# Seven block products for the queries, keys and values of the forgetting attention, in place of a product per 128 tokens

## The reference, cut to what matters

```python
h = rms_norm(x, norm_mix_g[l])                      # x: (1, 512, 1024)
(f_q, f_k, f_v, f_f, n_q, ...) = split_cols(h @ w_in[l])   # f_q, f_k, f_v: 512 columns each
qa = rms_norm(to_heads(f_q, FOX_HEADS), fox_q_g[l])  # 8 heads of 64
ka = rms_norm(to_heads(f_k, FOX_HEADS), fox_k_g[l])
va = to_heads(f_v, FOX_HEADS)
log_f = jax.nn.log_sigmoid(f_f.astype(jnp.float32) + b_forget[l])
out_a = from_heads(fox_attention(qa, ka, va, log_f)) @ w_fox_up[l]
```

## Time and profile before

| | |
|---|---|
| median of 3 runs | 1430.56 us (1430.36 to 1430.82) |
| the profiled execution | 1434.81 us, its span 1433.5 us |
| busy: PE, PEld, DVE, ACT, POOL | 95%, 55%, 40%, 24%, 25% of the span |
| PE products of whole tiles (L467), 320 passes | 142.7 us |
| PE block products (L1592), passes of 128x256, first group 288 | 65.0 us |
| POOL sums of blocks (L1400), groups of 56 and 28 | 72.9 and 36.8 us |

### The profile page before, as it was taken

How to read it: one execution, slowest core, us unless ns; L and a number is a source line. 1 busy time by engine, 2 the same in 40 slices (tenths; PEclk the granted TensorE clock), 3 DMA queues, 4 the chain that set the end, 5 groups by cost and what they waited for, 6 DMA issues and landing times. The chain is left out here.

```text
span 1433.5 us, 24217 instructions
## 1 busy us (share of the span) xinstructions
PE 1361.1 (95%) x10188; PEld 785.7 (55%) x10188; DVE 567.9 (40%) x1394; ACT 351.1 (24%) x832; POOL 359.9 (25%) x426
## 2 busy tenths in 40 slices
PE   7999999899999997999999979999999999999997
PEld 3545544567888645444444434456877545555543
DVE  3235423573141534521211133545459582333415
ACT  2225324553101011111111123354221301322221
POOL 3050402205372561122222120220232003111062
PEclk9999999999999997999999999999999999999999
DMA  6175013310222348899999991010140331300131
GB/s 213 56 275 203 1 61 88 139 42 5 102 75 86 136 162 296 314 375 356 382 379 380 387 336 63 15 67 2 59 176 30 85 122 39 127 3 17 56 122 59
DMA packets 99791, 210.95 MB, mean 147 GB/s; under 512 B 14613, under 2 KB 22640, under 8 KB 99552
## 3 DMA queue, kind: packets, MB, share of 16 engines
q1 hardware_dynamic: 87152, 171.39, 33.0%
q0 software_dynamic: 12528, 37.97, 7.9%
HBM read 188.88 MB, written 19.42 MB: 145 GB/s over the span
## 5 line engine op out<-in xcount | busy, mean ns | idle before, releaser
L467 PE MATMUL pb<-Wt,HT 128*128 128x512 f32 x320 | 142.7, 600 | 0.6 <-DMA Wt<-in_w_in_dram 0.6
L3708 PE MATMUL pb<-Wt,HT 128*128 128x512 f32 x256 | 117.8, 602 | 0.2 <-DVE AR L3799 0.2
L1400 POOL TENSOR_TENSOR AR<-Wt,AR 128x512 f32<-128x512 f32 x56 | 72.9, 1323 | 122.6 <-PE pb L1592 89.5
L467 PEld LDWEIGHTS pb<-Wt,HT 128*128 128x128 f32 x320 | 60.0, 192 | 70.6 <-issue 70.5
L766 ACT ACTIVATE AR<-AR,SM 128x512 f32<-128x512 f32 (+3 forms) x128 | 70.8, 554 | 62.3 <-DVE SM L724 61.5
L2266 PE MATMUL pb<-AR 128*64 128x512 f32 x256 | 85.0, 595 | 0.7 <-issue 0.7
L724 DVE CUSTOM_DVE_ANT_0 AR<-pb,AR 128x512 f32<-128x512 f32 (+3 forms) x128 | 58.3, 487 | 64.4 <-PE pb L678 63.9
L1400 POOL TENSOR_TENSOR AR<-Wt 128x512 f32<-128x512 f32 x28 | 36.8, 1333 | 166.8 <-DMA Wt<-in_w_in_dram 81.0
L3708 PEld LDWEIGHTS pb<-Wt,HT 128*128 128x128 f32 x256 | 46.4, 190 | 52.0 <-issue 49.2
L2266 PE MATMUL pb<-Wt,AR 128*64 128x512 f32 x192 | 70.8, 595 | 0.0
L678 PE MATMUL pb<-AR 64*128 64x512 f32 (+7 forms) x256 | 62.5, 493 | 7.9 <-DVE SM L724 5.0
(11 more groups left out here) (575 smaller groups left out, 2400.5 us busy)
## 6 DMA issues: line engine op xcount, KB each, us to landing
Wt<-in_w_in_dram SPq DMA_DIRECT2D x18, 2048.0 KB, 9.5
AR<-in_w_gate_dram SPq DMA_DIRECT2D x8, 2048.0 KB, 17.3
AR<-in_w_up_dram SPq DMA_DIRECT2D x8, 2048.0 KB, 16.0
AR<-in_w_down_dram SPq DMA_DIRECT2D x8, 2048.0 KB, 13.6
Wt<-in_w_gate_dram SPq DMA_DIRECT2D x6, 2048.0 KB, 15.3
Wt<-in_w_down_dram SPq DMA_DIRECT2D x6, 2048.0 KB, 12.4
Wt<-in_w_up_dram SPq DMA_DIRECT2D x6, 2048.0 KB, 22.4
ys<-AR POOLq DMA_DIRECT2D x2, 3072.0 KB, 24.8
```

The costliest lines, as they stand in the source:

```text
L467: r = mm(s[:, 0:n], lT[:, k, t * 128:(t + 1) * 128], w[:, k, c0:c0 + n], start=k == 0, stop=k == nk - 1)
L1400: r = gt.tensor_tensor(out[:, k:k + s, :], a[:, k:k + s, :], b[:, k:k + s, :], op)
L3708: r = mm(s, HT[:, k, t * 128:(t + 1) * 128], W.ap(("gate2", c, br))[:, k, :], start=k == 0, stop=k == 7)
```

## The change

Queries, keys and values become three units of `Quarters` (`fq7`, `fk7`, `fv7`, L1592 there L1720). The queries' weights are loaded first, in place of the values', and their first two products p1 and p2 stand between the turns of the first norm. The four quarters of the result (c11 of tokens 0 to 255 and columns 0 to 255, and so on) take the place of the four tiles in the head norm: the first is read from PSUM, the three others from SBUF, where DVE has put them. The norm's scratch moves. POOL gets 24 sums of blocks: the queries' and keys' before the running sums are stored, the values' after the clearing of rows and before the masks; one of the broadcasts and its masks move to the end. The weights' slots come free at other products.

```diff
-        for name in ("fox_v", "fox_q", "fox_k", "nsa_q", "nsa_kv"):
+        for name in ("fox_q", "fox_k", "fox_v", "nsa_q", "nsa_kv"):
             W.plan(name, 8, 512)
...
-            load("fox_v", wcols(a["w_in"][0], 1024, 512))
+            load("fox_q", wcols(a["w_in"][0], 0, 512))
...
         def norm1_pe():
-            pipe(ALLT, norm1.turn_pe, lambda t: fox_v_pe(t) if t < 2 else None)
+            norm1.turn_pe(0)
+            norm1.turn_pe(1)
+            for t in range(2):
+                norm1.turned(t, pe)
+            fq7.p1_pe()
+            norm1.turn_pe(2)
+            fq7.p2_pe()
+            norm1.turn_pe(3)
             columns_pe()
...
+        def block_norm_ve(u, tag, b, s):
+            turned = ("turn", tag, b - 2) if b > 1 else (("turn", "fq", b + 2) if tag == "fk" else None)
+            if b == 0:
+                ht8.norm_ve(P.ap(u.key("x")), P.free(u.key("x")), s, turned)
+            else:
+                ht8.norm_ve(flat((u.c12, u.c22, u.c21)[b - 1]), None, s, turned)
+
+        def fox_qkv_pe():
+            q, k, v = fq7, fk7, fv7
+            q.p5_pe()
+            gates_pe()
+            q.p6_pe()
+            block_turn_pe(q, "fq", 0)
+            q.p3_pe()
+            running_sums_pe()
+            q.p7_pe()
+            k.p1_pe()
+            q.p4_pe()
+            block_turn_pe(q, "fq", 1)
+            k.p5_pe()
+            block_turn_pe(q, "fq", 2)
+            k.p2_pe()
+            block_turn_pe(q, "fq", 3)
...
+            k.p6_pe()
+            k.p3_pe()
+            block_turn_pe(k, "fk", 0)
+            k.p7_pe()
+            v.p1_pe()
+            k.p4_pe()
+            block_turn_pe(k, "fk", 1)
+            v.p5_pe()
+            block_turn_pe(k, "fk", 2)
+            v.p2_pe()
+            block_turn_pe(k, "fk", 3)
+            v.p6_pe()
+            v.p3_pe()
+            v.p7_pe()
+            v.p4_pe()
...
+        def fox_qkv_ac():
...
+            block_norm_ac(k, 2)
+            block_norm_ac(k, 3)
+            block_turn_ac("fk", 1)
+            v.first_ac()
+            block_turn_ac("fk", 2)
+            v.c11_ac()
+            block_turn_ac("fk", 3)
...
+        def first_sums_po():
+            po.wait_ge(s_xn, 4)
+            def sums():
...
+                for t in ALLT:
+                    norm1.turned(t, po)
+                tiles_po(s1, a21, a22, ALU.add, s_hleft)
...
+            fq7.right_po(ahead=sums)
+            fk7.right_po()
```

More of the change, by code:

```diff
@@ L860, in forget_pe, with gates_pe @@
             W.last("gates", "gate_parts")
-            fox_v_pe(2)
+        def gates_pe():
             pe.wait_ge(*P.drained("gate_parts"))
-            s = P.take(pe, "S", "gates")
+            s = P.take(pe, "O", "gates")
             for t in ALLT:
@@ L969, in fox_qk_ve, with fox_qkv_ve @@
+        def fox_qkv_ve():
+            q, k, v = fq7, fk7, fv7
+            block_norm_ve(q, "fq", 0, -0.125)
+            q.p5_ve()
+            gates_ve()
+            q.p6_ve()
+            log_gates_ve()
+            q.c12_ve()
+            block_norm_ve(q, "fq", 1, -0.125)
+            running_sums_ve()
+            q.c22_ve()
+            block_norm_ve(q, "fq", 2, -0.125)
+            q.c21_ve()
+            block_norm_ve(q, "fq", 3, -0.125)
+            k.p5_ve()
             ve.wait_ge(*P.filled("cum_t"))
@@ L992, in fox_bias_po @@
                     gt.tensor_tensor(own, own, mid(C["causal"], 4), ALU.add).then_inc(s_bias, 1)
+            po.wait_ge(s_const, 16)
+            po.wait_ge(s_fb, 48)
+            for i in order_i[0:3]:
+                mask(i)
+            po.wait_ge(s_head, 6)
+            broadcast(1)
+            po.wait_ge(s_fb, 64)
+            mask(1)
         att = AttendPairs(scr2, small)
         def fox_pe():
-            for t in ALLT:
+            for b in range(4):
                 for tag in ("fq", "fk"):
-                    pe.wait_ge(*P.drained(("turn", tag, t)))
-                pe.wait_ge(*P.drained(("fox_v", t)))
+                    pe.wait_ge(*P.drained(("turn", tag, b)))
+            for bank in "xzy":
+                pe.wait_ge(*P.drained(fv7.key(bank)))
+            pe.wait_ge(*fv7.read(2))
             half = lambda x, hp: x[64 * hp:64 * hp + 64]
@@ L1538, in __init__ @@
                                                           for c in range(2) for k in range(2))
+                if isinstance(dst, tuple):
+                    self.c12, self.c22, self.c21 = dst
+                    return
                 lo, hi = slice(0, 256), slice(256, 512)
@@ L1672, in c21_ve @@
                     ve.wait_ge(*P.drained(self.key(bank)))
+        quarter_sems = s_part4, s_first4, s_read4, s_right4
+        first_lefts = [AR[:, 1024 * j:1024 * j + 1024].rearrange("p (k n) -> p k n", n=256) for j in range(4)]
+        ar = Place(AR, ARN, 16384)
+        first_use = dict(sems=(*quarter_sems, s_hleft), tokens=HT, weights=lambda tag: (tag, W.ap(tag)),
+                         lefts=first_lefts, rights=[ar.take(4, 256) for _ in range(3)],
+                         copies=[ar.take(2, 256) for _ in range(3)], late=None)
+        block = [AR[:, 25216 + 512 * j:25728 + 512 * j].rearrange("p (i n) -> p i n", n=256) for j in range(4)]
+        first7 = []
+        for n, (tag, dst) in enumerate((("fox_q", tuple(block[0:3])), ("fox_k", (block[3], block[0], block[1])),
+                                        ("fox_v", fv))):
+            first7.append(Quarters(tag, n, first_use, dst, True, first7[-1] if first7 else None))
+        fq7, fk7, fv7 = first7
         mix = Place(AR, ARN, base1).take(8, 512)
```

150 lines of the change are left out of this document (85 added, 65 removed).

## The result

| | before | changed |
|---|---|---|
| median (15 runs each) | 1430.56 us | 1438.9 us |
| range of the runs | 1425.74 to 1437.7 | 1433.87 to 1441.44 |
| profiled execution | 1434.8 us | 1433.87 us |

The ratio is 1.0055, with an interval of 1.0039 to 1.0071: the change makes the kernel **7.9 us slower** (5.6 to 10.2). That is the side on which the prediction put the most chance, but twice its +3.9 us, and just above its range. The profiled execution of the change is its fastest run, 5 us under its median, while the profile before is 4 us over its own, so their ends can't be set against each other. Their stages can.

A forecast was written before the change was run, and what follows sets the result against it. PE was taken to bound the projections' stage. Products and their short waits gave -2.5 us, POOL slowing DVE +5.5, the clock +0.9: +3.9 in sum, a median of 1434.5 us, range 1426.0 to 1438.0.

The forecast's parts named there:

- To the gates' products: Stretch up to the gates' products: start at 30.9 instead of 32.10, 1.2 us gained despite p1 starting late.
- From the gates to the scores: Nineteen products (65.6 us) replace ten tiles (68.7): 3.1 gained, against new waits of 0.8, 1.0 and 5.5 us.
- p4 of the queries: PE waits 2.0 us there, as DVE's norm of the queries' second quarter is slowed by POOL's sums.
- The stall of 3.0: PE waits 3.0 us before p2 of the values for ACT's copy, behind keys' norms slowed by POOL.
- The product of a quarter does wait: In the head norm, DVE's product of a quarter, both inputs in SBUF, waits for POOL: 1.2 us plus a little.
- half a fall: Clock cost of the new waits before the scores: 0.9 us, between no fall and two (3.6).
- the clock falls in each long wait: Rival: two clock falls at the new waits, +6.6 us, 1437.2; within the stalls' shared chance of 0.57.
- the fall at the scores as it is: At the first scores the clock falls as in the kernel before, a cost of 1.8 us in both.
- The faster rival: Rival: norms escape POOL and the scores start at full clock, -4.3 us, 1426.3; chance 0.18.
- Everything behind that point is the same in both kernels: From the first scores on, both kernels run alike; only the scores' start and the clock make a difference.
- Hidden norms: Rival: DVE's norms escape POOL or PE comes later, so the 5.5 us vanish: -2.5, 1428.1; chance 0.20.
- The values' sums did not come late: Rival claimed late sums on POOL's queue: p5 of the values waits 2 us, 1436.5 with the rest; chance 0.05.

The follow-up runs named there:

- tiny_sums: The changed kernel with POOL's 24 sums cut to eight columns of one block; first scores at 108.40 us, one run, no ratio.
- key_sums_late: The changed kernel with POOL starting the keys' sums only after DVE normed the queries' second quarter; ratio to the kernel before 1.0044.
- turn_early: The changed kernel with DVE writing tile 1 of the first norm before scaling tile 2; ratio to the kernel before 1.0031.
- after_pad209: The changed kernel with 209 more instructions on PE that only wait for something long there; ratio to the kernel before 1.0131.
- clear_late: The changed kernel with the values' sums split around stores, broadcasts and last head norm, masks and clearing behind them; ratio to the kernel before 1.0023.
- best1: The changed kernel with key_sums_late, turn_early and clear_late joined, tile 3 scaled earlier, values' p2 between p7 and p4; ratio to the kernel before 0.9963.
- before_gap: The kernel before with PE waiting for four chained POOL clearings ahead of the queries' last tile; ratio to the kernel before 1.0036.

## Why the prediction was right and wrong

**To the gates' products: the course right, the gain not shown.** I had 1.2 us gained. The five profiles of the kernel before (with and without padding or gap) start them at 29.8 to 33.0, the three of the change at 31.4, 30.6 and 32.7: 0.2 us sooner in the mean, in a spread of over 2 us. p1 waited 6.4 us and took its slow passes (5.24 in place of 3.45), as written; how long these take (5.2 to 6.7) makes much of the spread.

**From the gates to the scores: right in sum, by errors that cancelled.** The forecast was -3.1 + 0.8 + 1.0 + 5.5 = +4.2; the first profile has +3.8 (82.4 against 78.6). Part by part: the first sum 0.75 for 0.8; the end 0.73 for 1.0 (0.88 twice in place of 1.03); the last norm 0.18 for 0.2; p4 of the queries 1.16 for 2.0; p2 of the keys none for 0.3. The stall of 3.0 was there with 2.77, **but not where I had put it**: before p4 of the keys, not before p2 of the values. I had the values' sums begin at 79 and so took the keys' second quarter, normed from 76.9, as clear of POOL. I had read POOL's issues of the clearing as work that DVE doesn't feel. By themselves they nearly are (tiny_sums), but L400 started in them, with the full sums right behind, and was held for 2.79 us, to the end of the first sum operation. With PE late by that, the quarter behind it gave ACT's copy of p1 the time it needed (93.38 has no bracket). And the products took 3.45 to 3.55, some 1 us more over nineteen.

**The product of a quarter does wait: right.** I took 1.2 us and a little over its 0.69; it took 1.64 to 1.71, and 0.69 with the sums cut. The Trainium skill's rule in "SBUF — State Buffer", section "Who interferes with whom", on two inputs in SBUF is borne out by that pair of runs. L400 has only one input and was held longest; rows 7 had it already, with 1.15 us for L399. The same section says that a tensor_scalar can enter a mode that takes the port pair which DVE shares with GpSimd, and, as an inference, that GpSimd's making of DMA descriptors needs the write side of that pair. With issues alone the trace agrees in kind but not in size: 0.28 us in tiny_sums, ended with the issue. Why L400 wasn't let go between the issues and the sum in the changed kernel is not shown.

**The clock: both terms wrong, against each other.** For the new waits I took half a fall, 0.9 us. The wait of 2.8 us stands in five profiles (changed twice, key_sums_late, turn_early, after_pad209), and the clock fell behind it in four: p4 took 5.38 three times and 6.67 once. Against the first profile, which had no fall, the way from that p4 to the scores was 1.7 us longer three times, and 3.0 once: 1.6 in the mean over the five. So a fall there is the rule, and the single idle time of 1.80 without one was a poor guide for one of 2.8. The scores start at 113.74, 115.95 and 116.71 in the change's three profiles, 115.5 in the mean, against 110.8. Without a fall the first profile is +3.1 against its counterpart, where the sum without the clock was -2.5 + 5.5 = +3.0; in the mean it is +4.7 against the forecast's +3.9. The clock term is short by 0.7 of these 0.8. My rival "the clock falls in each long wait", 1437.2, was nearer to the result than my forecast, though only one of its two falls came: behind the wait of 1.16, which it had at 2.0, none did. The other term was "the fall at the scores as it is". It went away in seven of nine profiles of kernels with block products, for 1.0 us in the mean (seven of them without padding), which takes back the 0.7 that the first term was short of. That the two cancel is luck. The faster rival had that half right, but not for its reason: the three idle times in a row were still there.

**"Everything behind that point is the same in both kernels": the step that failed.** It was used without a row for it. The work is the same, its time isn't. Of +7.9 us, 4.7 stand at the scores and 3.2 behind them (profiles for the one, medians for the other, so each to within 1 us or so). As 1.0 is gained at the first scores, 4.2 are lost further on. clear_late, best1, turn_early and key_sums_late agree with that: they end 4.4, 3.1, 3.2 and 3.0 us later than their scores would have it. Shown is the largest part of it: 303 instructions more on PE move its pauses, two from 1200 to 1345 become three, and that stretch takes 2.5 us longer in the mean, 1.4 without a fall of the clock and 3.3 with one. Padding alone took it away in both kernels where it was tried on the change, and brought 0.8 net in the kernel before. The 0.37 near 229 came in all changed kernels alike (0.8 in tiny_sums); the padding stood behind that place, so its cause isn't tested. **The other 1.3 us stay open.** Low clock behind the scores varies too much between profiles of one kernel to settle it: about 280 to 310 us, kernels that are the same up to there had 3.4 to 14 us of it.

**The rivals.** Hidden norms needed DVE to escape POOL; it escaped in neither of the two norms that the products waited for. The faster side needed the same, beside the full clock at the scores, which did come. The values' sums did not come late for their products: p5 of the values had no wait.

## What to carry to other kernels

An eighth less work in the products is worth nothing while the short elementwise work in front of the next product lies beside another engine's stream: the change became a gain of 5 us only when POOL's sums, clearing and masks were moved out of the norms' way, tile 1 was made ready when the first product could use it, and a product was put between p7 and p4. When a product becomes half as long, list for each one which elementwise result it needs, and check what POOL does over exactly that time, up to the end of the operation that it begins next. And where effects are a few microseconds, compare at several points of the trace: "the same code behind it" is an assumption.

## What was new of the hardware

- A 128x8 TENSOR_SCALAR on DVE took 2.79 us beside POOL's DMA issues with a full sum right behind, 0.28 beside such an issue with a tiny sum behind, 0.17 alone.
- A single idle time of PE of 2.8 us was followed by a low clock in four of five profiles; those of 1.16 us in the same kernels were not, nor was the one of 2.02 in before_gap, whose next tile took its usual time.
- PE pauses for 0.8 to 1.5 us (once per run for 2.0 to 2.7) at places set by the number of instructions before them: 47 more moved the pauses by 23 or 24 products and turned two into three from 1200 to 1345; 256 more left them where they were. They showed only in rows of tiny products, and in four of seven profiles of the changed kernels a fall of the clock began within some 2 us of one.
- The fall of the clock at the first scores, there in five of five profiles of the kernel before, came in two of nine with block products, at nearly the same idle times.
- An instruction on PE that only waits, for something long there, takes 0.10 us.
